# Order of VectorE and ScalarE work at the start of three feed-forward stages, and the first output rows scaled during the last chain of products

## The chip, the cores and the metric

One core of one Trainium2 chip runs the whole program. The metric is device time in microseconds (us); a kernel's time is the median of its runs.

## The reference, cut to what matters

A float32 model of three transformer blocks over one sequence of 256 tokens of width 1024. Each block is a mixer (stick-breaking attention, a latent attention with top-k selection, then sliding-window attention beside a gated recurrence) followed by a feed-forward stage, and the program ends with a norm over each token's row. The two places that the change touches:

```python
# feed-forward, blocks 0 and 1 (gate and val both pass the convolution)
h = rms_norm(x, norm_ffn[i]) * (1.0 + sc2) + sh2
u = h @ w_up                                   # 1024 -> 2 * 2816
y = conv_b + sum(up[:, j:j + S] * conv_w[j] for j in range(3))   # causal, along the tokens
gate, val = jnp.split(y, 2, axis=-1)
x = x + g2 * ((jax.nn.silu(gate) * val) @ w_down)
# block 2: only the gate passes the convolution
u, v = jnp.split(h @ w_up, 2, axis=-1)
x = x + gate_f * ((jax.nn.silu(causal_depthwise_conv(u, conv_w, conv_b)) * v) @ w_down)
return rms_norm_2(x, final_norm_g)             # y = x * rsqrt(mean(x * x) + EPS) * gain, row by row
```

## The kernel before

Activations lie transposed: xT holds 8 chunks of 128 channels by 256 tokens. Weights stream from HBM into six slots of 128 x 8 x 256 float32 (1 MB each), on SyncE's queue, in program order: the load of a slot waits for `slot_used` of that slot, and what stands behind it on the queue waits too. Every engine runs its own list of instructions, written out by hand and ordered by semaphores.

**Start of a feed-forward stage, `ffn(l)` for l = 0, 1, 2.** The output projection of the mixer before it (`out_projection`) makes eight chunks of xT in four blocks n = 0 to 3; `OUT_SLOTS[l]` names the slots of its four weight blocks. VectorE adds each block into xT, ScalarE makes xg (chunks of x times the gain, `xg_ready`) and squares, VectorE sums the squares (`sum_after_out`, ending in part_sum, `part_ready`). The first hidden columns don't wait for the norm: TensorE multiplies the unnormalised xg (`up_raw`, line 793, 64 matmul instructions) and in the midst of it adds up the squares over the partitions (`norm_sum`, line 760). From that ScalarE makes rstd (L1528, L1529), and VectorE multiplies the raw products by it afterwards (`normalise`, L2058 to L2063). In the meantime VectorE makes h from x (`norm`, L1978), ScalarE adds the shift (`shifted`, L1535, `h_ready`).

All later hidden columns are made from h in a fast form of 2 x 2 block products with seven products in place of eight (`up_seven`, L850). It needs sums of weights (`weight_sums(n, halves)`, four VectorE operations of 128 x 1024 at L2017, L2018, L2020, L2021: halves 0 are the first two, halves 1 the last two) and sums of inputs (`input_sums`, L2030 to L2036). Partial results lie in PSUM; ScalarE copies them on as starting values of the next products (`seed`, L1573, three per half step, and zeroing at L1590), and TensorE waits for each seed (`seeds_ready`). A step n has two half steps, j_odd 0 and 1; place p = 2n + j_odd numbers them, in tables `place_of`. After each half step VectorE adds two parts (`collect`, L2048), does the convolution (`chunk` on VectorE, L2081, L2086, L2091, `conv_ready`), ScalarE the silu (`chunk` on ScalarE, L1570, `silu_ready`), VectorE the product with the other half (`product`, L2106, L2111 or L2123). For l < 2 TensorE multiplies each such product by w_down at once (`down`, L896), 16 matmul instructions after every half step. For l = 2 the products are kept and multiplied at the end, in four blocks of seven chains (`down_blocks`, `chain`, L971, 22 matmul instructions each).

For l < 2 the first silu stands on ScalarE before the eight `shifted` operations, and the second between the first and the second seed of place 0. For l = 2 the first silu stands in the same place, the second after place 0. TensorE begins place 0 only when `normalise(1)` has read the second raw product (`was_read(3)`, a wait at the matmul of L865).

**The end.** VectorE adds each chain's result into xT (`take`, L2154). TensorE transposes finished pieces of xT back to rows (`turn`, L959, into PSUM banks 4 to 7), ScalarE squares and sums them row by row (`squares_of`, L1853, `ss_ready`), takes the root (`token_root`, L1860, `rtok_ready`), VectorE its reciprocal, and `token_rows` (L2666, 128 x 512 each) scales the rows by it and by the gain: three quarters of the output by VectorE, the third (rows 128 to 255, first half) by ScalarE (L1871). SyncE stores the four quarters (L598).

## Time and profile before

| what | value |
| --- | --- |
| median of 3 runs | 1099.87 us (1098.5 to 1101.79) |
| the profiled execution | 1098.37 us, of which the span from first to last instruction 1096.5 us |
| TensorE (PE) matmul busy | 1073.6 us, 98% of the span |
| VectorE (DVE) busy | 788.8 us, 72% |
| ScalarE (ACT) busy | 332.0 us, 30% |
| mean granted clock of TensorE | 0.999 of full speed |
| DMA | 234.79 MB, mean 214 GB/s |

A page of the profile gives busy time by engine and by group of instructions. Four other views are used below: the waits (which engine waited for which line, how long in total, how often, the longest), the timeline (instructions in order of time, like ones merged, with the idle time of their engine before them in brackets and what ended it), the windows (busy time of an engine in a stretch), and the chain of waits (the work that ended last, followed back). PEld is TensorE's weight load, which runs ahead of the matmul that it belongs to. SPq are DMAs issued by SyncE.

### The profile page before, as it was taken

Reading aid. Unit: us, or ns where it says so; the run is one execution under the profiler, and the core shown is the slowest. Engines: PE = TensorE matmul, PEld = TensorE weight load, DVE = VectorE, ACT = ScalarE, POOL = GpSimd, SP = SyncE. Lnnn points to the kernel's source line nnn. Section 1 sums busy time; section 2 is a strip of 40 time slices with the busy share of each in tenths; the row PEclk is TensorE's granted clock in tenths of the full one; section 3 lists DMA queues with packets and bytes.
Section 4 is the critical chain, followed back from the end, with each engine's and each line's share of the span. In section 5 each row is a group of like instructions: output and inputs, shape, how many; then the busy total and the mean of one; then the engine's idle time right before and its main releaser. Section 6 shows DMA issues by size and latency. Waiting matters only on the chain.

```text
span 1096.5 us, 18062 instructions
## 1 busy us (share of the span) xinstructions
PE 1073.6 (98%) x7396; PEld 972.1 (89%) x7396; DVE 788.8 (72%) x1359; ACT 332.0 (30%) x783; POOL 24.5 (2%) x83
## 2 busy tenths in 40 slices
PE   7999999999999999999999999999999999999997
PEld 4788888999999977888899999998889889999997
DVE  2477768888898848544779889887474288887755
ACT  3243324111111245663511111117343342222101
POOL 1000240000000000000000000000000000000000
PEclk9999999999999999999999999999999999999999
DMA  9899936898878662381868878774432165953411
GB/s 347 275 385 343 316 106 249 297 319 282 319 276 300 191 77 77 98 258 57 299 214 323 309 280 304 263 251 151 154 116 77 46 204 171 290 184 106 151 62 39
DMA packets 163011, 234.79 MB, mean 214 GB/s; under 512 B 8770, under 2 KB 137842, under 8 KB 162930
## 3 DMA queue, kind: packets, MB, share of 16 engines
q1 hardware_dynamic: 162572, 233.54, 63.2%
q8 instruction: 58, 0.95, 0.4%
q14 instruction: 24, 0.19, 0.1%
q10 hardware_dynamic: 357, 0.12, 0.0%
HBM read 232.19 MB, written 1.44 MB: 213 GB/s over the span
## 4 chain that ended last, share of the span: by engine, by line
PE 88%; DVE 8%; ACT 2%; issue 1%; ACTq 0%; DMA 0%; DVEq 0%
PE PS L850 34%; PE PS L780 13%; PE PS L896 13%; PE PS L808 7%; PE PS L971 6%; PE PS L1096 3%; PE PS L772 1%; PE PS L1358 1%; DVE hT L1978 1%; PE PS L793 1%; PE PS L701 1%; PE PS L1441 1%; DVE scratch L2400 1%; PE PS L1300 1%; PE PS L1049 1%
## 5 line engine op out<-in xcount | busy, mean ns | idle before, releaser
L780 PE MATMUL PS<-hT,slots 128*128 128x256 f32 x752 | 165.3, 380 | 0.8 <-ACT hT L1535 0.8
L780 PEld LDWEIGHTS PS<-hT,slots 128*128 128x128 f32 x752 | 142.1, 190 | 21.7 <-issue 2.9
L896 PE MATMUL PS<-act,slots 128*128 128x256 f32 x704 | 159.8, 380 | 0.4 <-DVE act L2123 0.4
L1902 DVE SCALAR_TENSOR_TENSOR ada_acc<-ada_slots,cond,ada_acc 128x1024 f32<-128x1024 f32 x119 | 152.4, 1280 | 4.8 <-DMA ada_slots<-in_ada_w 0.5
L896 PEld LDWEIGHTS PS<-act,slots 128*128 128x128 f32 x704 | 130.5, 190 | 18.9 <-issue 1.6
L1573 ACT ACTIVATE PS<-PS 128x128 f32<-128x128 f32 x180 | 53.5, 297 | 299.7 <-PE PS L850 299.7
L850 PE MATMUL PS<-oT,slots 128*128 128x128 f32 x960 | 126.9, 275 | 2.0 <-ACT PS L1573 2.0
L850 PE MATMUL PS<-hT,slots 128*128 128x128 f32 x960 | 127.0, 275 | 0.0
L850 PEld LDWEIGHTS PS<-hT,slots 128*128 128x128 f32 x960 | 119.6, 192 | 2.4
L850 PEld LDWEIGHTS PS<-oT,slots 128*128 128x128 f32 x960 | 116.8, 192 | 2.3 <-issue 2.3
L850 PE MATMUL PS<-oT,scratch 128*128 128x128 f32 x960 | 117.1, 275 | 0.0
L850 PEld LDWEIGHTS PS<-oT,scratch 128*128 128x128 f32 x960 | 112.0, 192 | 0.1
L808 PE MATMUL PS<-oT,slots 128*128 128x256 f32 x384 | 85.2, 380 | 0.0
L808 PEld LDWEIGHTS PS<-oT,slots 128*128 128x128 f32 x384 | 72.2, 190 | 10.7 <-issue 1.3
L850 PE MATMUL PS<-hT,scratch 128*128 128x128 f32 x480 | 63.4, 275 | 0.0
L850 PEld LDWEIGHTS PS<-hT,scratch 128*128 128x128 f32 x480 | 58.4, 192 | 0.0
L793 PE MATMUL PS<-xg,slots 128*128 128x257 f32 (+1 forms) x256 | 57.6, 381 | 0.0
L793 PEld LDWEIGHTS PS<-xg,slots 128*128 128x128 f32 (+1 forms) x256 | 47.7, 187 | 8.1 <-issue 0.8
L2081 DVE TENSOR_SCALAR ffn_work<-PS,pcol 128x256 f32<-128x256 f32 x100 | 50.7, 540 | 2.2
L1590 ACT ACTIVATE PS<-ident 128x128 f32<-128x128 f32 x60 | 16.6, 278 | 108.6 <-DVE PS L2048 108.6
L2048 DVE TENSOR_TENSOR PS<-PS,k_sq 128x256 f32<-128x256 f32 x54 | 23.2, 430 | 35.1 <-PE PS L850 33.4
L2086 DVE SCALAR_TENSOR_TENSOR ffn_work<-PS,pcol,ffn_work 128x255 f32<-128x255 f32 x100 | 44.2, 475 | 0.7
(347 smaller groups left out, 1337.0 us busy)
## 6 DMA issues: line engine op xcount, KB each, us to landing
ada_slots<-in_ada_w SPq DMA_DIRECT2D x144, 512.0 KB, 8.6
slots<-in_ffn_w_up SPq DMA_DIRECT2D x44, 1024.0 KB, 11.9
slots<-in_ffn_w_down SPq DMA_DIRECT2D x22, 1024.0 KB, 5.0
slots<-in_w_up SPq DMA_DIRECT2D x22, 1024.0 KB, 5.2
slots<-in_sb_w_in SPq DMA_DIRECT2D x11, 1024.0 KB, 13.2
slots<-in_w_in SPq DMA_DIRECT2D x11, 1024.0 KB, 5.3
slots<-in_dsa_w_in SPq DMA_DIRECT2D x10, 1024.0 KB, 5.4
ada_slots<-in_w_down SPq DMA_DIRECT2D x2, 2816.0 KB, 12.4
```

The costliest lines, as they stand in the source:

```text
L780: last = mm(PS[:, bank, half * T:half * T + T], slot[s][:, k, m * P:(m + 1) * P], x[:, k, :], start=k == 0, stop=k == KC - 1)
L793: last = mm(PS[0:n, bank, 0:T + 1], slot[s][:, k, m * P:m * P + n], xg[:, k, 0:T + 1], start=k == 0, stop=k == KC - 1)
L808: last = mm(PS[:, 2 * OUT_UNITS[l][n] + m, half * T:half * T + T], slot[OUT_SLOTS[l][n]][:, k, m * P:(m + 1) * P], oT[:, k, :], start=k == ...
L850: last = mm(dst, w[:, k, cols], x[:, k, :], start=fresh and k == 0, stop=k == HALF - 1, skip_group_check=True)
L896: last = mm(PS[:, c // 2, (c % 2) * T:(c % 2) * T + T], w[:, j_odd * D + c * P:j_odd * D + (c + 1) * P], act[:, j_odd, :], start=start and ...
L971: last = mm(PS[:, PRODUCT_BANKS[n % 4], 0:P], w[:, i, :], x[:, i, :], start=i == 0, stop=i == PAIRS - 1, skip_group_check=True)
L1096: last = mm(PS[:, 2 + tt, 0:SLAB], hT[:, k, tt * P:(tt + 1) * P], slot[s][:, k, :], start=k == 0, stop=k == KC - 1)
L1573: act_e.activation(dst.rearrange("p (x t) -> p x t", x=copies), stem(at).unsqueeze(1).to_broadcast([P, copies, P]), ACT.Copy).then_inc(see ...
L1902: ins = dve.scalar_tensor_tensor(dst, ada_slot[k][:, :], c, dst, ALU.mult, ALU.add)
L2048: dve.tensor_tensor(second, partial, at.z.unsqueeze(1).to_broadcast([P, 2, P]), ALU.add)\
L2081: dve.tensor_scalar(dst, ps[:, 0:T], dcol(f"conv2_{l}", j + off), dcol(f"convb_{l}", j + off), ALU.mult, ALU.add).then_inc(dve_step, 1)
L2086: dve.scalar_tensor_tensor(dst[:, 1:T], ps[:, 0:T - 1], dcol(f"conv1_{l}", j + off), dst[:, 1:T], ALU.mult, ALU.add).then_inc(dve_step, 1)
```

## The change

Three edits for the feed-forward starts, and one group for the end.

1. ScalarE, l < 2: the second silu of the stage (`chunk(1)`) moves from between the first and second seed of place 0 to behind its third seed. For l = 2 both first silus stand there, behind the eight `shifted` operations and the seeds of place 0.
2. VectorE, l = 2: the first half of `weight_sums(2, 0)` moves ahead of the last block of the output projection (`before_last`), the second half behind `sum_after_out`. Then `norm(1)` whole, `input_sums`, both `normalise` and `chunk`, the first half of `weight_sums(2, 1)`, both `product`. The third row of `OUT_SLOTS` changes from (2, 3, 4, 5) to (3, 4, 2, 5): slots 3 and 4, which hold the weights that `weight_sums(2, 0)` reads, are let go one block earlier.
3. TensorE, l = 2: the wait for the second `normalise` ahead of place 0 goes.
4. The end: TensorE transposes piece (7, 1) before the last three products of the last chain and no longer behind it. VectorE takes the first reciprocal and scales the first quarter before it takes the last chain, and adds up the square sums before it scales the second quarter. ScalarE issues the store of the quarter that it scales itself.

```diff
-OUT_SLOTS = ((3, 4, 5, 2), (3, 4, 5, 2), (2, 3, 4, 5))
+OUT_SLOTS = ((3, 4, 5, 2), (3, 4, 5, 2), (3, 4, 2, 5))
@@ SyncE, stores
-            for n, (made, count) in enumerate(((o_ready, 1), (o_ready, 2), (o_scaled, 1), (o_ready, 3))):
+            for count, n in enumerate((0, 1, 3)):
@@ TensorE, up_seven and down_blocks
-                    if n == 0 and not j_odd:
+                    if l < 2 and n == 0 and not j_odd:
                         was_read(3)
...
-                        if i == PAIRS - 1 and late is not None:
+                        if i == late_at and late is not None:
                             late()
...
+                def turn_corner():
+                    pe.wait_ge(x_turned, 11)
+                    pe.wait_ge(ss_ready, 3)
+                    turn(7, 1, signal=True)
...
-                    chain(b, 6, s_sum[2], acts[:, :, 1, P:T])
-                pe.wait_ge(x_turned, 11)
-                pe.wait_ge(ss_ready, 3)
-                turn(7, 1, signal=True)
+                    chain(b, 6, s_sum[2], acts[:, :, 1, P:T], late=turn_corner if b == 3 else None, late_at=8)
@@ ScalarE, ffn
-                chunk(0)
-                skip(2)
+                    chunk(0)
+                    skip(2)
                 shifted(3)
...
-                    if l < 2:
+                    if l < 2 and p:
                         chunk(1 - odd)
                         skip(3 - odd)
...
-                    if l == 2:
+                    if p == 0:
+                        for raw_odd in (0, 1) if l == 2 else (1,):
+                            chunk(raw_odd)
+                            skip(2 + raw_odd)
+                    elif l == 2:
                         chunk(1 - odd)
...
             act_e.activation(oT_flat[:, 1024:1536], oT_flat[:, 1024:1536], ACT.Copy, scale=rtok[:, 1:2]).then_inc(o_scaled, 1)
+            act_e.wait_ge(o_scaled, 1)
+            act_e.dma_start(out[0, P:2 * P, 0:512], oT_flat[:, 1024:1536]).then_inc(out_stored, 16)
@@ VectorE
                 for n in range(4):
+                    if n == 3 and before_last is not None:
+                        before_last()
...
+                        else:
+                            dve.wait_ge(rtok_ready, 1)
+                            link(dve.reciprocal(rtok[:, 0:1], rtok[:, 0:1]))
+                            token_rows(0, 0)
                         take(b, 6, (0, 1, 2))
...
+                if l == 2:
+                    weight_sums(2, 0, (1,))
+                    norm(1)
+                    input_sums()
+                    for odd in range(2):
+                        normalise(odd)
+                        chunk(odd, odd, raw[:, odd, 0, :], raw[:, odd, 1, :])
+                    weight_sums(2, 1, (0,))
+                    for odd in range(2):
+                        product(odd, normalised=True, j=odd)
+                    last_chunks()
+                    return
...
-            out_projection(2, units=OUT_UNITS[2])
+            out_projection(2, units=OUT_UNITS[2], before_last=lambda: weight_sums(2, 0, (0,)))
             ffn(2)
...
-            dve.wait_ge(rtok_ready, 1)
-            link(dve.reciprocal(rtok[:, 0:1], rtok[:, 0:1]))
-            token_rows(0, 0)
-            token_rows(0, 1)
             dve.wait_ge(ss_ready, 5)
             dve.tensor_tensor(ss[:, 1, 0:1], ss[:, 1, 0:1], ss[:, 1, 2:3], ALU.add).then_inc(ss_eps_ready, 1)
+            token_rows(0, 1)
```

ScalarE at the start of the first feed-forward stage, before: L1590 zeroes, L1573 are the seeds, L1596 copies the fifth product, L1570 is the silu.

```order
L1590 ACTIVATE PS<-ident 128x128 [waits unit_read2]
L1573 ACTIVATE PS<-PS 128x128 [waits stem_full0]
L1570 ACTIVATE ffn_work<-ffn_work 128x256 [waits conv_ready]
L1573 ACTIVATE PS<-PS 128x128 [waits stem_full0]
L1596 ACTIVATE k_sq<-PS 128x128
L1573 ACTIVATE PS<-PS 128x256 [waits stem_full0]
```

And the same place after the change, where lines stand two further down (L1572 is the silu).

```order
L1592 ACTIVATE PS<-ident 128x128 [waits unit_read2]
L1575 ACTIVATE PS<-PS 128x128 [waits stem_full0] x2
L1598 ACTIVATE k_sq<-PS 128x128
L1575 ACTIVATE PS<-PS 128x256 [waits stem_full0]
L1572 ACTIVATE ffn_work<-ffn_work 128x256 [waits conv_ready]
```

The silu went from between the seeds to behind them.

VectorE where the last feed-forward stage begins, before: L1995 adds the output projection into xT, L1952 sums squares, L2017 to L2021 are the weight sums, L2058 the first normalise.

```order
L1995 SCALAR_TENSOR_TENSOR xT<-PS,mod,xT 128x256 [waits unit_full0]
L1995 SCALAR_TENSOR_TENSOR xT<-PS,mod,xT 128x256
L1995 SCALAR_TENSOR_TENSOR xT<-PS,mod,xT 128x256 [waits unit_full1]
L1995 SCALAR_TENSOR_TENSOR xT<-PS,mod,xT 128x256
L1952 TENSOR_TENSOR hT<-hT 128x512 [waits sq_ready]
L1952 TENSOR_TENSOR hT<-hT 128x512 [waits sq_ready,dve_step] x2
L1952 TENSOR_TENSOR part_sum<-hT 128x256 [waits dve_step]
L2017 TENSOR_TENSOR scratch<-slots 128x1024 [waits w_sums_used,slot_loaded4,slot_loaded3]
L2018 TENSOR_TENSOR slots<-slots 128x1024 [waits dve_step]
L2020 TENSOR_TENSOR scratch<-scratch,slots 128x1024 [waits dve_step]
L2021 TENSOR_TENSOR scratch<-slots,scratch 128x1024 [waits dve_step]
L2058 TENSOR_TENSOR fm<-PS,rstd 128x256 [waits rstd_ready,unit_full2]
```

After the change (L2005 into xT, L1960 sums of squares, L2024 to L2028 weight sums, L1986 norm).

```order
L2005 SCALAR_TENSOR_TENSOR xT<-PS,mod,xT 128x256 [waits unit_full0]
L2005 SCALAR_TENSOR_TENSOR xT<-PS,mod,xT 128x256
L2024 TENSOR_TENSOR scratch<-slots 128x1024 [waits w_sums_used,slot_loaded4,slot_loaded3]
L2025 TENSOR_TENSOR slots<-slots 128x1024 [waits dve_step]
L2005 SCALAR_TENSOR_TENSOR xT<-PS,mod,xT 128x256 [waits unit_full1,dve_step]
L2005 SCALAR_TENSOR_TENSOR xT<-PS,mod,xT 128x256
L1960 TENSOR_TENSOR hT<-hT 128x512 [waits sq_ready]
L1960 TENSOR_TENSOR hT<-hT 128x512 [waits sq_ready,dve_step] x2
L1960 TENSOR_TENSOR part_sum<-hT 128x256 [waits dve_step]
L2027 TENSOR_TENSOR scratch<-scratch,slots 128x1024
L2028 TENSOR_TENSOR scratch<-slots,scratch 128x1024 [waits dve_step]
L1986 SCALAR_TENSOR_TENSOR hT<-xT,gain,rstd 128x256 [waits rstd_ready]
```

Two weight sums, with their wait for the loads of slots 3 and 4, now stand ahead of the last two additions into xT, and the norm stands ahead of the first normalise.

ScalarE behind the seeds of place 0 in that stage, after the change (before it, the table for the silu was loaded right behind the root, L1529):

```order
L1531 ACTIVATE rstd<-rstd 128x256 [waits act_step]
L1537 ACTIVATE hT<-hT,mod 128x256 [waits scaled_ready] x8
L1592 ACTIVATE PS<-ident 128x128 [waits unit_read1]
L1575 ACTIVATE PS<-PS 128x128 [waits stem_full0] x2
L1598 ACTIVATE k_sq<-PS 128x128
L1575 ACTIVATE PS<-PS 128x256 [waits stem_full0]
L1572 ACT_TABLE_LOAD
L1572 ACTIVATE ffn_work<-ffn_work 128x256 [waits conv_ready] x2
L1592 ACTIVATE PS<-ident 128x128 [waits unit_read2]
```

The table load and two silus now stand between place 0's last seed and the zeroing that place 1 waits for.

## Rows read from the trace of the kernel before

**Rows 1.** The waits, TensorE's own: us in total, times, longest

```profile
PE PS L850 <- ACT PS L1573: 2.0, 2, 1.0
...
PE PS L865 <- DVE cc L2059: 1.4, 1, 1.4
```

**Rows 2.** Timeline, first feed-forward stage, place 0: start, duration, engine, line

```profile
184.73 0.42 ACT L1570 ACTIVATE ffn_work<-ffn_work 128x256 f32<-128x256 f32 x1 [2.70 <-DVE ffn_work L2091]
...
185.19 0.43 DVE L2123 TENSOR_TENSOR act<-ffn_work 128x256 f32<-128x256 f32 x1
...
185.46 1.13 PE L850 MATMUL PS<-oT,slots 128*128 128x128 f32 x8 [1.05 <-ACT PS L1573]
...
188.10 3.33 PEld L896 LDWEIGHTS PS<-act,slots 128*128 128x128 f32 x16
```

**Rows 3.** Windows, place 0 of stages one and two, TensorE: stretch, length, busy, clock

```profile
180.56:191.66 11.10, 10.05 (x74) 1.00 0.22 71
543.04:554.07 11.03, 10.05 (x74) 1.00 0.22 68
```

**Rows 4.** Chain of waits, the next half step: start, duration, piece

```profile
191.94 6.25 PE PS L850 x56
198.19 3.46 PE PS L896 x16
```

**Rows 5.** Timeline, start of the last feed-forward stage

```profile
874.67 0.88 DVE L1995 SCALAR_TENSOR_TENSOR xT<-PS,mod,xT 128x256 f32<-128x256 f32 x2 [1.73 <-PE PS L808]
...
878.12 0.88 DVE L1995 SCALAR_TENSOR_TENSOR xT<-PS,mod,xT 128x256 f32<-128x256 f32 x2 [2.58 <-PE PS L808]
...
881.29 0.42 DVE L1952 TENSOR_TENSOR part_sum<-hT 128x256 f32<-128x256 f32 x1
881.63 1.22 DVE L2017 TENSOR_TENSOR scratch<-slots 128x1024 f32<-128x1024 f32 x1
...
882.25 0.59 PE L760 MATMUL PS<-part_sum,restart 128*128 128x256 f32 x2
...
893.81 0.22 PE L865 MATMUL PS<-ident_b 128*128 128x128 bf16 x1 [1.43 <-DVE cc L2059]
```

**Rows 6.** SyncE's timeline at the load of slot 3

```profile
871.64 0.37 SPq L437 DMA_DIRECT2D slots<-in_w_up  x1
```

**Rows 7.** DMA issues of that stretch: count, size, median us to landing

```profile
slots<-in_w_up SPq DMA_DIRECT2D x1, 1024.0 KB, 5.1
...
ada_slots<-in_final_norm_g SPq DMA_DIRECT2D x1, 512.0 KB, 8.9
```

**Rows 8.** Timeline, ScalarE and TensorE up to place 1 of the last stage

```profile
883.38 1.28 ACT L1529 ACT_TABLE_LOAD   x1
...
884.67 0.42 ACT L1529 ACTIVATE rstd<-rstd 128x256 f32<-128x256 f32 x1
...
898.73 0.37 ACT L1573 ACTIVATE PS<-PS 128x256 f32<-128x256 f32 x1 [1.34 <-PE PS L850]
...
899.32 0.27 ACT L1590 ACTIVATE PS<-ident 128x128 f32<-128x128 f32 x1
...
901.32 1.95 PE L850 MATMUL PS<-oT,scratch 128*128 128x128 f32 x16
```

**Rows 9.** Chain of waits, the end

```profile
1087.15 0.22 PE PS L959 x2
...
1089.86 0.36 DVE xT L2154
```

**Rows 10.** Timeline, the end: ScalarE, VectorE

```profile
1088.13 0.29 ACT L1860 ACTIVATE rtok<-ss 128x1 f32<-128x1 f32 x1
...
1090.56 1.41 DVE L2666 SCALAR_TENSOR_TENSOR oT<-PS,rtok,ada_slots 128x512 f32<-128x512 f32 x2
...
1092.13 0.29 ACT L1860 ACTIVATE rtok<-ss 128x1 f32<-128x1 f32 x1 [0.94 <-DVE ss L2674]
```

**Rows 11.** SyncE's timeline at the last two stores

```profile
1093.40 0.81 SPq L598 DMA_DIRECT2D out<-oT  x2
```

More of the change, by code:

```diff
@@ L593, in _ @@
                 load_down_block(b)
-            for n, (made, count) in enumerate(((o_ready, 1), (o_ready, 2), (o_scaled, 1), (o_ready, 3))):
+            for count, n in enumerate((0, 1, 3)):
                 tt, lo = n // 2, n % 2 * 512
-                sp.wait_ge(made, count)
+                sp.wait_ge(o_ready, count + 1)
                 sp.dma_start(out[0, tt * P:(tt + 1) * P, lo:lo + 512],
@@ L962, in turn, with chain @@
                         last.then_inc(turn_full, 1)
-                def chain(b, q, w, x, late=None):
+                def chain(b, q, w, x, late=None, late_at=PAIRS - 1):
                     n = 7 * b + q
@@ L2001, in out_projection, with weight_sums @@
                         after()
+            def weight_sums(l, n, halves=(0, 1)):
+                g, v = LAST_SETS[(n + 1) % 3] if l == 2 else (3 - 3 * (n % 2), 4 - 3 * (n % 2))
+                gate, val, ws = slot[g], slot[v], w_sum[n % 2]
+                if 0 in halves:
+                    for s, landed in zip((g, v), up_landed[l, n + 1]):
+                        dve.wait_ge(slot_loaded[s], landed)
+                    used = bk("w_sums_used")
+                    if used.n >= 2:
+                        dve.wait_ge(w_sums_used, used.value(1))
+                    used.next()
+                    link(dve.tensor_tensor(ws[:, 0, :, :], val[:, 0:HALF, :], val[:, HALF:KC, :], ALU.add))
+                    link(dve.tensor_tensor(val[:, 0:HALF, :], gate[:, 0:HALF, :], val[:, 0:HALF, :], ALU.subtract))
+                if 1 in halves:
+                    link(dve.tensor_tensor(ws[:, 1, :, :], ws[:, 0, :, :], gate[:, 0:HALF, :], ALU.subtract))
+                    dve.tensor_tensor(ws[:, 2, :, :], gate[:, HALF:KC, :], ws[:, 1, :, :], ALU.subtract)\
+                        .then_inc(w_sums_ready, 1)
@@ L2003, in ffn, with token_rows @@
+            def token_rows(tt, half):
+                lo = half * 512
+                dve.scalar_tensor_tensor(oT_flat[:, tt * D + lo:tt * D + lo + 512], PS[:, 4 + 2 * tt + half, :], rtok[:, tt:tt + 1],
+                                         final_g[:, lo:lo + 512], ALU.mult, ALU.mult).then_inc(o_ready, 1)
             def ffn(l):
                 both = l < 2
[L2006 to L2022 removed]
@@ L2054, in normalise @@
                     full(2 + odd)
-                    if not odd:
+                    if not odd and both:
                         dve.wait_ge(rstd_ready, bk("rstd_ready").next())
```

36 lines of the change are left out of this document (6 added, 30 removed).

## The prediction, made before the changed kernel was run

> **What bounds the kernel now.** I read TensorE's own waits first, because its matmuls fill nearly the whole span and every microsecond that it stands still is one that a reordering can give back. What is to be seen there is how little is left: the longest items that this change touches are 2.0 us in two waits of line 850 for a seed of ScalarE, and one of 1.4 us of line 865 for the second normalise on VectorE [rows 1]. Then the timeline around each of these, to see what the releasing engine did just before; and last the chain at the end of the program, where TensorE has finished and only short operations of VectorE and ScalarE, then the stores, follow one another. So the change can win at three starts of a stage and at the end, and each of these stands on the path: the stages between are TensorE's, and their loads are let go by TensorE's own progress, so what is won early should be kept.
>
> **Stages one and two (edit 1).** At place 0 of the first stage ScalarE makes its first seed, then waits 2.70 us for the convolution, does the silu from 184.73 on for 0.42 us, and only then the second seed; TensorE stands idle 1.05 us and goes on at 185.46 [rows 2]. The two waits together are 2.0 us [rows 1], so the second stage has about 1.0. With the silu behind the third seed the second one is made as soon as its product is there, and the wait goes. How much that is: at least the idle time, 1.05 and 1.0. At most the difference between this half step and an undisturbed one. The half step lasts 11.10 us in the first stage and 11.03 in the second [rows 3], an undisturbed one 6.25 + 3.46 = 9.71 [rows 4], which leaves 1.39 and 1.32, and in these lies the one small matmul of line 865 that only the first half steps have, some 0.1. The ends of matmuls in a profile are drawn late by the depth of the pipe, so the truth is between; I take 1.15 and 1.1.
>
> What is late next: the silu itself, and with it the product that the second `down` needs. The product before the third seed starts at about 184.3 in place of 185.46 and ends by about 185.4; the seed takes 0.37 (the same form as in [rows 8]), the silu 0.42, VectorE's product 0.43 with 0.04 of handing over [rows 2], together about 186.7. TensorE loads the first weights of `down` at 188.10 now [rows 2], then at 186.7 to 186.95. That is level to 0.2 us of slack. If I am a little wrong here it costs one or two tenths in each stage, no more, because the sum can't end later than this chain. VectorE has nothing else due in this gap.
>
> **Last stage (edits 2 and 3).** What goes is the wait for the second normalise, 1.43 us of idle TensorE before 893.81 [rows 5]; drawn late as above, up to 1.6. The next places take their banks one after another and don't need both normalises at once.
>
> What comes in its place is a wait on a load. The first two weight sums now stand ahead of the last two additions into xT. They need slots 3 and 4. With the new order of slots the load of slot 4 is issued when TensorE begins the third output block, which is when slot 3 is let go now, at 871.64 [rows 6]. It takes 5.1 us to land [rows 7], so it is there at 876.74. VectorE is free at 874.67 + 0.88 = 875.55 [rows 5], waits 1.2 us, and does two operations of 1.22 us with 0.04 between them [rows 5], until 879.3. Now the last additions start at 878.12. They start 1.2 us later. Behind them on VectorE are queued the sums of squares, and behind these TensorE's line 760; on ScalarE the last two chunks of xg, which TensorE's raw products eat one after another. The end of part_sum is at 881.29 + 0.42 = 881.71 and TensorE takes it at 882.25 [rows 5]: 0.54 of slack, of which some 0.15 is handing over. So 1.2 - 0.4 = 0.8 us of new idle time inside the raw products. All that follows from rstd fits well: the eight norms, eight shifts and four input sums are done some microsecond before TensorE has finished the raw products, because nothing of normalise or convolution stands between them any more.
>
> Then ScalarE. The table for the silu was loaded while it waited for VectorE; now it stands behind the last seed of place 0, with two silus behind it and then the zeroing without which TensorE can't make the second product of place 1. From TensorE's start at 893.81: the last seed ends at 898.73 + 0.37 = 899.10, which is 5.3 us after it; a table load is 1.28 and the next operation starts 0.01 after it (883.38 to 884.67) [rows 8]; two silus at 0.42 each and the zeroing 0.27, the last overlapping somewhat: 5.3 + 1.3 + 0.7 + 0.3 = 7.6. TensorE wants it at 901.32 - 893.81 = 7.5 [rows 5, 8], less the handing over of about 0.15 to 0.2. A new wait of about 0.3. VectorE is not late there: two times normalise and convolution are done before the table is.
>
> Sum of the stage: 1.5 - 0.8 - 0.3 = 0.4 us. Its bounds are 1.6 (neither new wait) and below nothing, -0.5 (the load a microsecond later than 5.1).
>
> The Trainium skill, "ScalarE: Activation LUTs", section "What ACT_TABLE_LOAD costs", says that a switch of table takes about 1.38 us of draining beside its 1.28, 2.66 us in all. By that the new wait would be 1.7 and not 0.3, the stage would lose 1.0 and the sum below would be 2.2. The row speaks against it: the operation behind the load starts 0.01 us after its 1.28 [rows 8], and I go by the row.
>
> **The end (edit 4).** The square sums of the last piece are there at 1092.13 - 0.94 = 1091.19, but the root starts only at 1092.13, because VectorE first scales two quarters (1.41 us from 1090.56) and then adds up the sums that the root needs [rows 10]. After the change the first quarter is scaled while the last chain runs: its root is started at 1088.13 and takes 0.29, reciprocal and scaling fit before VectorE takes the last chain at 1089.86 [rows 9, 10]. The sum stands ahead of the second quarter, and that quarter is done before the next reciprocal. So 0.94 goes, less 0.05 of handing over from the squares. Against it the transposition inside the last chain puts the chain's end 0.11 later (two take 0.22 [rows 9]); half of that is returned because the squares of that piece are no longer what the last transposition waits for. Net 0.85. The two last stores are issued in 0.81 us from 1093.40 on, one behind the other [rows 11]; with ScalarE issuing one, the fourth is up to 0.4 sooner, at worst nothing if their data share the engines anyhow. I take 0.1, nearer nothing, since two quarters still have to pass.
>
> **The sum.** 1.15 + 1.1 + 0.4 + 0.85 + 0.1 = 3.6 us. The profiled execution, 1098.37 us with a span of 1096.5, becomes 1094.8 with a span of 1092.9. That execution is 1.5 us below the median of the runs shown, and within their spread; taken off the median: 1099.87 - 3.6 = 1096.3 us, or 0.33%. A measurement of this kernel can tell about 0.3%, 3.3 us, from no change.
>
> **Rivals.**
> - *No new wait in the last stage* (slot 4 lands before VectorE is free, or table and silus hide): for it, all three are a matter of tenths; against it, the load is issued too late by 1.2 us unless TensorE runs the blocks differently. 1.15 + 1.1 + 1.5 + 0.95 = 4.7, so 1095.2 us. Chance 0.10.
> - *The last stage gives more back than it wins.* The zeroing of place 1 waits for a table load that can't run ahead. If switching holds ScalarE a microsecond longer than the row of the load itself, or VectorE's second convolution is late, the stage ends at -1.0: gain 2.2, 1097.7 us. For it: 0.3 us is already missing by my own count, and every tenth more goes straight onto TensorE. Chance 0.15.
> - *The early gain isn't kept.* In stages one and two the silu is late for `down` and the wait only moves there, or a later piece that hangs on loads takes it back: only the end is won, and little more, gain about 1.3, 1098.6 us. For it: the slack of 0.0 to 0.2. Against it: the old wait was for something ready only at 184.73, and the new chain ends two microseconds later but 1.4 us before TensorE's present 188.10. Chance 0.18.
> - *Slower: the load of slot 4 is late.* VectorE is an engine in order, and with the weight sums ahead of the additions into xT every microsecond by which that load lands later than 5.1 stops TensorE for a microsecond. It decides from 5.1 + 3.6 = 8.7 us on. There is a row for that: a load of half the size issued on the same queue while others were under way took 8.9 [rows 7]; it would give +0.2 us, 1100.1. Against it: at 871.64 the queue is empty, since what stands ahead was issued one block earlier. Chance 0.05.
> - The forecast itself: 0.52.
>
> **How the numbers follow.** The forecast's own span is a gain of 2.7 to 4.5, 1095.4 to 1097.2; of its 0.52 about 0.40 lies over 3.3. Faster by over 0.3%: 0.40 + 0.10 = 0.50. Within 0.3%: 0.12 + 0.15 + 0.18 = 0.45. Slower: 0.05, half of it past 0.3% by the row, all of it counted. The range takes in the first three rivals and the scatter of a median of a few runs, whose single runs lie 1.4 us below and 1.9 above the present one: 1094.6 to 1099.2.
>
> **What would show it right or wrong.** In TensorE's waits the two of line 850 for the seed are gone, and no wait of `down` for VectorE's product has come at its place; half step 0 of the first two stages lasts 9.8 to 9.9 us. In the last stage the wait for the normalise is gone, VectorE's first weight sum there starts about 1.2 us after it is free and names the load as its releaser, TensorE idles about 0.8 us in the raw products, and 0.2 to 0.4 us at place 1 for ScalarE's zeroing, with the table load directly ahead. At the end the second root starts within 0.1 us of the last squares, and the last scaling ends 0.85 us sooner after the last chain. Wrong, if TensorE's idle time at place 1 is over a microsecond, if the first weight sum waits more than 2 us, or if the sum of these places is right and the time doesn't follow.

## The result, and the profile after

The changed kernel takes 1094.01 us (median of 4 runs, 1093.74 to 1094.63) where the kernel before takes 1099.69 beside it (4 runs, 1098.5 to 1101.79). The ratio is 0.9947, with a 95% interval of 0.993 to 0.9964: faster by 0.53%. The prediction was 1096.3 us with a range from 1094.6 to 1099.2. The direction is right, the gain is larger than forecast, and the time lies 0.6 us below the range. Two of all the runs counted below were far off (one of e1 at 1119.86 us with a granted clock of 0.948, one of the kernel before at 2882.23 us); the ratios leave them out and the medians hardly feel them.

The profiled execution took 1093.74 us with a span of 1091.9. TensorE is busy for 1071.2 us of it (1073.6 before).

TensorE's waits after, longest first (us in total, times, longest). The two of line 850 for a seed and the one of line 865 for the second normalise [rows 1] are gone: the list goes on with waits of 1.1 us and less, none of them of lines 850 or 865.

```profile
PE PS L1030 <- DMA oT<-in_x: 3.6, 1, 3.6
PE PS L1021 <- DMA ffn_work<-in_c: 3.0, 1, 3.0
PE PS L1037 <- DMA ffn_work<-in_ffn_norm_g: 1.7, 1, 1.7
PE PS L721 <- DVE mod L1946: 1.2, 1, 1.2
```

The timeline of place 0 in the first feed-forward stage (start, duration, engine, line), to be held against [rows 2]:

```profile
184.89 0.37 ACT L1575 ACTIVATE PS<-PS 128x256 f32<-128x256 f32 x1 [1.34 <-PE PS L850]
185.17 0.41 ACT L1572 ACTIVATE ffn_work<-ffn_work 128x256 f32<-128x256 f32 x1
...
185.58 1.06 PE L850 MATMUL PS<-oT,slots 128*128 128x128 f32 x8
185.61 0.42 DVE L2139 TENSOR_TENSOR act<-ffn_work 128x256 f32<-128x256 f32 x1 [0.97 <-ACT ffn_work L1572]
186.37 0.73 PEld L896 LDWEIGHTS PS<-act,slots 128*128 128x128 f32 x4
```

The silu (line 1572) now stands directly behind the third seed (line 1575), and VectorE's product ends at 186.03, 0.34 us before TensorE loads the first weights of `down`. So nothing waits there. The windows of the same half step, which answer to [rows 3] (stretch, length, then TensorE's busy time):

```profile
180.12:189.93 9.81, 9.81 (x74) 9.31 (x73) 8.13 (x19) 1.68 (x6) 0.00 (x0) 1.00 0.24 75
541.31:551.13 9.82, 9.82 (x74) 9.31 (x73) 8.07 (x19) 1.68 (x6) 0.00 (x0) 1.00 0.25 79
```

TensorE is busy in the whole of both, and they are 1.29 and 1.21 us shorter than before.

The timeline at the start of the last stage, which answers to the first rows of [rows 5]:

```profile
873.84 1.22 DVE L2024 TENSOR_TENSOR scratch<-slots 128x1024 f32<-128x1024 f32 x1 [1.23 <-issue]
...
874.98 4.85 PE L793 MATMUL PS<-xg,slots 128*128 128x257 f32 x20
875.10 1.22 DVE L2025 TENSOR_TENSOR slots<-slots 128x1024 f32<-128x1024 f32 x1
...
876.35 0.88 DVE L2005 SCALAR_TENSOR_TENSOR xT<-PS,mod,xT 128x256 f32<-128x256 f32 x2
...
877.82 1.60 PEld L793 LDWEIGHTS PS<-xg,slots 128*128 128x128 f32 x8 [0.48 <-ACT xg L1551]
...
880.00 0.70 PE L760 MATMUL PS<-part_sum,restart 128*128 128x256 f32 x2 [0.17 <-DVE part_sum L1960]
```

VectorE is idle for 1.23 us ahead of its first weight sum, which the view puts down to "issue". The chain of waits has the load of slot 4 right ahead of it (start, duration, piece):

```profile
868.70 3.91 DMA slots<-in_w_up
872.61 1.23 issue
873.84 1.24 DVE scratch L2024
...
876.35 0.04 DVE xT L2005
```

From the issue at 868.70 to VectorE's start at 873.84 it is 5.14 us, and that load took 5.1 us to land (the four of this stretch 5.0 to 5.2). So VectorE waited for the load, though the view doesn't name it. The additions into xT (line 2005) then start 1.37 us after TensorE's first raw product; before they started 0.20 us after it (878.12 in [rows 5], against this line of the timeline before):

```profile
877.92 4.50 PE L793 MATMUL PS<-xg,slots 128*128 128x257 f32 x20
```

TensorE pays at two places. Its weight loads wait 0.48 us for ScalarE's xg, and the row of 20 matmuls takes 4.85 us in place of 4.50. Then it waits for part_sum, so that line 760 starts 5.02 us after the first raw product and no longer 4.33 (882.25 - 877.92). The other new wait is at place 1 (the same timeline, further on), against [rows 8]:

```profile
894.84 0.37 ACT L1575 ACTIVATE PS<-PS 128x256 f32<-128x256 f32 x1 [1.34 <-PE PS L850]
...
895.23 1.28 ACT L1572 ACT_TABLE_LOAD   x1
...
896.43 0.22 PE L865 MATMUL PS<-ident_b 128*128 128x128 bf16 x1
...
896.52 0.72 ACT L1572 ACTIVATE ffn_work<-ffn_work 128x256 f32<-128x256 f32 x2
...
897.15 0.26 ACT L1592 ACTIVATE PS<-ident 128x128 f32<-128x128 f32 x1
897.47 2.05 PE L850 MATMUL PS<-oT,scratch 128*128 128x128 f32 x16
```

The table load, two silus and the zeroing (line 1592) follow each other without a gap, and TensorE starts the product behind the zeroing 0.98 us after the eight before it (896.49), where one place earlier it is 0.95, and its 16 matmuls take 2.05 in place of 1.95. That is the whole of the new wait.

The end, timeline, against [rows 9, 10, 11]. The store is ScalarE's own (ACTq):

```profile
1084.90 0.75 DVE L2034 SCALAR_TENSOR_TENSOR oT<-PS,rtok,ada_slots 128x512 f32<-128x512 f32 x1
...
1086.22 0.35 DVE L2170 SCALAR_TENSOR_TENSOR xT<-PS,mod,xT 128x128 f32<-128x128 f32 x1 [0.57 <-PE PS L971]
...
1087.22 0.19 ACT L1859 ACTIVATION_READ_ACCUMULATOR hT<-PS 128x1 f32 x1
1087.45 0.29 ACT L1866 ACTIVATE rtok<-ss 128x1 f32<-128x1 f32 x1
...
1087.98 0.75 DVE L2034 SCALAR_TENSOR_TENSOR oT<-PS,rtok,ada_slots 128x512 f32<-128x512 f32 x1
1088.73 0.39 ACTq L1879 DMA_DIRECT2D out<-oT  x1
```

The first quarter is scaled before the last chain is taken, and the second root starts 0.04 us after the sum of its squares has been read out (1087.22 + 0.19), with no idle bracket. Before, it started 0.94 us late [rows 10].

**Where the gain sits.** The first half steps of a stage each begin with a small matmul of line 865, and the distances between the starts of these differ between executions by a hundredth or two. Only where a load is waited for do they differ more: the 15.09 of the third row is 15.15 in e4, and 15.26 and 15.24 in e7 and e10, which have the same program there. So the trace gives the gain of each part nearly free of the scatter of whole times (us; a "place" is such a start):

| from, to | before | after | gain |
|---|---|---|---|
| stage one, place 0 to 1 | 11.10 | 9.81 | 1.29 |
| stage two, place 0 to 1 | 11.03 | 9.82 | 1.21 |
| last stage, first raw product to place 0 | 15.89 | 15.09 | 0.80 |
| last stage, place 0 to 1, and 1 to 2 | 6.50, 6.37 | 6.36, 6.50 | 0.01 |
| the pair of turns in the last chains, to the span's end | 9.34 | 8.50 | 0.84 |
| stage one, place 0, to the span's end | 915.93 | 911.78 | 4.15 |

The change is worth 4.15 us in the traces, against 3.6 in the prediction, and the medians lie 5.7 apart. The first question of the experiments is what the other 1.5 us are.

### The profile page after: what moved, and what is told of

It is laid out like the page before. It is cut to its first block, busy times and chain, and to the rows that moved or that the text cites. A ratio compares the mean times of both kernels' runs of the same rounds, so it can differ in the third digit from the quotient of the medians.

```text
span 1091.9 us, 18061 instructions
## 1 busy us (share of the span) xinstructions
PE 1071.2 (98%) x7396; PEld 971.0 (89%) x7396; DVE 789.0 (72%) x1359; ACT 331.9 (30%) x783; POOL 23.9 (2%) x83
## 3 DMA queue, kind: packets, MB, share of 16 engines
HBM read 232.19 MB, written 1.44 MB: 214 GB/s over the span
## 4 chain that ended last, share of the span: by engine, by line
PE 88%; DVE 5%; SPq 4%; ACT 1%; DMA 1%; issue 1%; DVEq 0%
PE PS L850 34%; PE PS L896 13%; PE PS L780 12%; PE PS L808 6%; PE PS L971 6%; PE PS L793 4%; PE PS L1098 2%; SPq L437 2%; PE PS L1360 1%; SPq L447 1%; PE PS L701 1%; SPq L504 1%; PE PS L1443 1%; DVE scratch L2428 1%; DMA ada_slots<-in_ada_w 1%
```

## The experiments

In each, "the places" are the distances of the table above, and the range behind a ratio is its 95% interval. Times of the kernel before, run beside the changed ones on the same chip, are given with each group.

**Parts 1 to 4: each part alone, and all again.** The kernel before beside these took 1098.97 us (median of 27 runs).

e1 is the kernel before with only the silu of place 0 moved behind the seeds in stages one and two:

```diff
-                    if l < 2:
+                    if l < 2 and p:
                         chunk(1 - odd)
                         skip(3 - odd)
...
+                    if l < 2 and p == 0:
+                        chunk(1)
+                        skip(3)
```

> Edit 1 alone (the second silu of stages one and two behind the third seed). Theory A, the sum of places: in the trace of the changed kernel TensorE is 1.29 us ahead after place 0 of stage one and 1.22 after that of stage two, so this kernel alone is 2.5 us faster than before and place 0 of both stages lasts 9.8 us from start to start. Theory B, something beside the places: the measured gain of the whole change is 5.7 us by the medians and the places show 4.2, so one of its parts carries 1.5 us more than its place shows; if it is this one, the time falls by 4 us while the places show 2.5.

Measured: 1096.39 us (11 runs), ratio 0.9975 (0.9966 to 0.9985), 2.6 less than before. The half steps are 9.82 and 9.82 us, stage one to the span's end 913.45 (2.48 less). The last stage is that of before, its wait included. This part holds more than half of the gain of the places, and it is kept to the end of the program.

e2 is the changed kernel with the first part and the end put back, so only the last stage is new (order of slots, weight sums ahead of the last additions, both input sums and normalises in a row, no wait for bank 3):

```diff
-OUT_SLOTS = ((3, 4, 5, 2), (3, 4, 5, 2), (2, 3, 4, 5))
+OUT_SLOTS = ((3, 4, 5, 2), (3, 4, 5, 2), (3, 4, 2, 5))
...
-                    if n == 0 and not j_odd:
+                    if l < 2 and n == 0 and not j_odd:
                         was_read(3)
...
+            out_projection(2, units=OUT_UNITS[2], before_last=lambda: weight_sums(2, 0, (0,)))
```

> Edits 2 and 3 alone (order of VectorE and ScalarE at the start of the last feed-forward stage, slot order, TensorE's wait gone). Theory A: 0.8 us faster, TensorE 0.8 ahead at place 2 of that stage, with a wait of VectorE for the load of slot 4 of about 1.2 us and idle time of TensorE of about 0.65 us in the raw products. Theory B, if this part carries the remainder: 2.3 us faster with 0.8 at the place.

Measured: 1097.87 us (11 runs), ratio 0.9997 (0.9988 to 1.0006), the median 1.1 less than before. By the ratio that is no clear difference; by the places, which tell more here, stage one to the span's end is 915.15, 0.78 less.

e3 is the kernel before with only the end changed (first quarter and turn inside the last chain, sum ahead of the second quarter, one store from ScalarE):

```diff
-                    chain(b, 6, s_sum[2], acts[:, :, 1, P:T])
+                    chain(b, 6, s_sum[2], acts[:, :, 1, P:T], late=turn_corner if b == 3 else None, late_at=8)
...
+                            token_rows(0, 0)
...
+            act_e.dma_start(out[0, P:2 * P, 0:512], oT_flat[:, 1024:1536]).then_inc(out_stored, 16)
```

> Edit 4 alone (the end: corner transposed inside the last chain, first quarter scaled early, square sums first, one store issued by ScalarE). Theory A: the last scaling ends 0.9 us earlier after the last chain and the span is 0.8 us shorter, since the time from the last scaling to the end of the program is 0.1 longer than before. Theory B, if this part carries the remainder: 2.3 us faster with 0.8 at the place.

Measured: 1097.55 us (11 runs), ratio 0.999 (0.9981 to 0.9999), the median 1.4 less. Stage one to the span's end is 915.04, 0.89 less. The three parts add up in the places: 2.48 + 0.78 + 0.89 = 4.15, the same as all together. None of them takes from another.

e4 is the changed kernel once more, with no line edited.

> The changed kernel once more, unaltered. Theory A: the places give 4.2 us and the rest of the 5.7 us between the medians is the scatter of the start (before 160 us the one profiled execution of before was 0.45 us behind that of the changed kernel, with the first 40 products at half the pace), so with more runs the difference settles at 4 to 4.6 us. Theory B: it stays at 5.5 us or more, and something beside the places is faster in every run.

Measured: 1094.2 us (5 runs), ratio 0.9962 (0.9949 to 0.9975), 4.8 between the medians and 4.2 by the ratio; stage one to the span's end 911.79. The changed kernel came back at its time, and the kernel before did not: its median was 1099.87 of the three runs shown and 1099.69 of the first four, but 1098.97 of these 27, 1098.58 of ten and 1098.63 of nine later on. So about 1 us of the 5.7 was a few high runs of the kernel before. Some 0.5 us are left: the later runs of before have a median of 1098.66 us (45 runs, without the one far off), the nine of the changed kernel 1094.10, which is 4.56 apart. The runs' spans, from first to last instruction, are 1096.4 and 1092.3 us in the median, 4.1 apart, which agrees with the places. The rest lies outside the span. In those 45 runs the time is longer than the span by 1.72 to 2.87 us (median 2.41), in the nine by 1.70 to 1.90. It goes with the end: in e3's 11 runs it is 1.75 to 1.85, while in e1 and e2, which have the old end, it goes up to 2.80 and 2.47. Issuing a store from ScalarE isn't the reason, since with all stores on SyncE (e7, below) it is 1.72 to 1.80 in four runs. Which other part of the new end does it stays open; no trace shows what lies outside the span.

**The two new waits of the last stage.** The kernel before beside these took 1098.58 us (10 runs).

e5 is the changed kernel with all four operations of the first weight sums behind the sums of squares:

```diff
-                    weight_sums(2, 0, (1,))
+                    weight_sums(2, 0)
...
-            out_projection(2, units=OUT_UNITS[2], before_last=lambda: weight_sums(2, 0, (0,)))
+            out_projection(2, units=OUT_UNITS[2], before_last=None)
```

> The changed kernel with one part put back: all four operations of the first weight sums of the last stage stand behind the sums of squares, so that nothing waits for slot 4 ahead of the last additions into xT. Theory A (the raw products lose their time to the load): VectorE's last additions start about 1.2 us earlier, TensorE's distance from the first raw product to the half step at place 0 falls from 15.09 to about 14.4 us (-0.6 to -0.8). Theory B (what holds the raw products is the order of ScalarE and the sums themselves, and the load only happens to lie beside them): the distance stays within 0.15 of 15.09. Either way the second VectorE operation of norm comes up to 1.5 us later and may be missed at place 1: if so the distance from place 0 to place 1 goes from 6.36 to 6.5 or more. One look, no timing; the distances between places hardly differ between executions.

Measured: from the first raw product to place 0 it is 14.30 us, 0.79 less than in the changed kernel; place 0 to 1 stays at 6.36 and place 1 to 2 at 6.50. One run took 1093.47 us. The timeline shows why: the additions start 0.20 us after TensorE's first raw product, as before, and neither wait is left in the 20 products.

```profile
875.65 4.50 PE L793 MATMUL PS<-xg,slots 128*128 128x257 f32 x20
875.85 0.88 DVE L2005 SCALAR_TENSOR_TENSOR xT<-PS,mod,xT 128x256 f32<-128x256 f32 x2 [2.58 <-PE PS L808]
...
879.98 0.38 PE L760 MATMUL PS<-part_sum,restart 128*128 128x256 f32 x1
```

The two weight sums by themselves would have been out of the way in time: without the wait they end at 876.32 - 1.23 = 875.09 us in the changed kernel, and the additions are due at 874.98 + 0.20. So theory A holds, waiting for the load cost 0.79 us (up to 0.96 by the executions of e7 and e10), and that VectorE's weight sums now end 8.71 us after the first raw product in place of 7.37 costs nothing.

e6 is e5 with ScalarE's table of the silu loaded ahead of the first seed of the last stage:

```diff
                     chunk(0)
                     skip(2)
+                else:
+                    act_e.preload_act_table(ACT.Silu)
                 shifted(3)
```

> As the one above (the first weight sums behind the sums of squares), and ScalarE loads the table for the silu before the first seed of the last stage, in place of between the last seed of place 0 and the first silu, where TensorE waits for the zeroing behind them. Theory A (both new waits are what I named): 0.6 to 0.8 us less in the raw products and 0.1 to 0.2 less at place 1, so place 2 comes 0.7 to 0.95 us sooner after the first raw product than in the changed kernel (27.95 us there), and the time is 0.7 to 1.0 us below it, near 1093.4 where before is 1098.5 to 1099. Theory B (the table load, 1.28 us, can't be hidden anywhere in ScalarE's row, it only delays the first seed): place 0 takes over 0.3 us longer than in the one above, and the time is within 0.3 us of the changed kernel.

Measured: first raw product to place 0 14.30 us, then 6.36 and 6.36; in all 0.93 less than the changed kernel. Time 1093.47 us (5 runs, 1092.88 to 1094.26), ratio 0.9955 (0.9942 to 0.9967). ScalarE now has 1.59 us to spare behind the zeroing, where it had 0.22:

```profile
894.52 0.75 ACT L1572 ACTIVATE ffn_work<-ffn_work 128x256 f32<-128x256 f32 x2
...
895.18 0.26 ACT L1594 ACTIVATE PS<-ident 128x128 f32<-128x128 f32 x1
...
897.03 0.26 ACT L1575 ACTIVATE PS<-PS 128x128 f32<-128x128 f32 x1 [1.59 <-PE PS L850]
```

Theory A holds by the places: the table's wait at place 1 was worth 0.14 us, the load's wait 0.79. By the places this is also the best version run, 5.14 us below the kernel before (stage one to the span's end 910.79). The median of the times is 0.5 to 0.7 below the changed kernel's (1094.01 and 1094.2), less than the 0.7 to 1.0 expected and within the scatter of the start.

**The slower rival, with its price.** e8 is the changed kernel with the old order of slots, so that slot 4 is let go one block later:

```diff
-OUT_SLOTS = ((3, 4, 5, 2), (3, 4, 5, 2), (3, 4, 2, 5))
+OUT_SLOTS = ((3, 4, 5, 2), (3, 4, 5, 2), (2, 3, 4, 5))
```

> The changed kernel with the old order of slots in the third output projection (2, 3, 4, 5), so that slot 4 is let go one output block later (about 3.45 us by the profile of before), while its weight sums still stand ahead of the last additions. This is the slower rival at its full price. Theory A (TensorE pays for each microsecond by which the load comes later than VectorE is free): VectorE's wait ahead of the first weight sum grows from 1.23 to about 4.7 us, and TensorE's distance from the first raw product to place 0 from 15.09 to about 18.5 us. Theory B (TensorE has other raw work beside it that hides a part): the wait grows as said, the distance by less than 2.5 us. One look, no timing.

Measured: VectorE waits 4.86 us ahead of the first weight sum, 3.63 more than in the changed kernel. From the first raw product to place 0 it is 19.97 us, 4.88 more. The wait came as theory A said, but both theories priced the distance too low. One run took 1099.1 us; stage one to the span's end is 916.64, 0.71 more than before. So the rival was real: with that one tuple left as it was, the change would have been no gain by the places. The timeline and the windows (length, TensorE and weight loads busy, ..., granted clock third from the end) show where the 1.25 us beyond the longer wait come from:

```profile
878.11 1.23 DVE L2024 TENSOR_TENSOR scratch<-slots 128x1024 f32<-128x1024 f32 x1 [4.86 <-issue]
...
882.10 2.78 PE L793 MATMUL PS<-xg,slots 128*128 128x257 f32 x8 [3.72 <-ACT xg L1551]
```

```profile
880.00:882.00 2.00, 0.00 (x0) 0.00 (x0) 1.96 (x4) 0.46 (x2) 0.00 (x0) 1.00 1.10 347
882.00:883.00 1.00, 0.90 (x4) 0.78 (x5) 0.79 (x2) 0.98 (x4) 0.00 (x0) 1.00 1.10 349
883.00:884.00 1.00, 1.00 (x5) 0.80 (x4) 0.90 (x2) 1.00 (x1) 0.00 (x0) 0.59 1.10 396
884.00:885.00 1.00, 1.00 (x4) 0.79 (x3) 1.00 (x2) 0.27 (x1) 0.00 (x0) 0.50 0.50 197
...
886.00:887.00 1.00, 1.00 (x5) 0.86 (x4) 0.61 (x1) 0.98 (x2) 0.00 (x0) 0.70 0.00 0
```

After 3.72 us of idle time TensorE was granted 0.50 of its clock, the 1.2 GHz level, from about 883.4 to 886.6, while it was already at work again. These eight products took 2.78 us, where the same eight took 2.00 in e4.

**The wait that was removed.** e9 is the kernel before with only the wait for bank 3 gone, VectorE's order untouched. The kernel before beside it and beside the next two took 1098.63 us (9 runs).

```diff
-                    if n == 0 and not j_odd:
+                    if l < 2 and n == 0 and not j_odd:
                         was_read(3)
```

> The kernel before with one thing gone: in the last stage TensorE doesn't wait at place 0 for bank 3, the bank of the second normalise. Everything else, the order of VectorE and ScalarE too, is that of before. Theory A (the 1.43 us wait is an order of waiting, and can be dropped by itself): the distance from the first raw product to place 0 falls from 15.89 to about 14.4 us, and the time is 1.4 us below before. Theory B (VectorE's order, where the second normalise comes behind the first convolution, makes the wait come back one step on, at the second product of place 0 or at place 1): place 2 comes less than 0.7 us sooner after the first raw product than before (28.76 us). If B holds, the new order of VectorE was needed to keep the gain.

Measured: the first raw product to place 0 falls to 14.30 us, 1.59 less; place 0 to 1 rises to 8.09, 1.59 more. To place 2 it is 28.75 us against 28.76. One run took 1098.65 us. TensorE's timeline and VectorE's:

```profile
891.80 0.22 PE L865 MATMUL PS<-ident_b 128*128 128x128 bf16 x1
894.46 2.02 PE L850 MATMUL PS<-oT,scratch 128*128 128x128 f32 x16 [1.49 <-DVE oT L2030]
```

```profile
892.42 0.75 DVE L2058 TENSOR_TENSOR fm<-PS,rstd 128x256 f32<-128x256 f32 x2
...
893.66 0.69 DVE L2030 TENSOR_TENSOR oT<-hT 128x512 f32<-128x512 f32 x1
```

Theory B holds. The wait for the second normalise stood in front of one for the input sums (line 2030), which VectorE makes only behind that normalise. In the changed kernel they come at 886.14, ahead of both normalises. With that order the 1.59 us are a gain (e5); removing the wait alone gives nothing.

**The store.** e7 is the changed kernel with all four stores on SyncE:

```diff
-            act_e.wait_ge(o_scaled, 1)
-            act_e.dma_start(out[0, P:2 * P, 0:512], oT_flat[:, 1024:1536]).then_inc(out_stored, 16)
```

> The changed kernel with all four output stores on SyncE again, in the order of before. Theory A (the two last stores end together whoever issues them; the prediction's 0.1 us isn't there): from the end of the last scaling to the end of the span 3.05 to 3.2 us, as the 3.17 of the changed kernel and the 3.09 of before. Theory B (a second issuing engine is worth what I gave it): 3.25 to 3.6 us. The time is no help here, since the difference looked for is 0.1 us.

Measured: 1093.98 us (4 runs). The last scaling starts here and is over at 1089.92, and the span ends at 1093.0:

```profile
1089.17 0.75 DVE L2032 SCALAR_TENSOR_TENSOR oT<-PS,rtok,ada_slots 128x512 f32<-128x512 f32 x1
```

From there to the span's end it is 3.08 us, against 3.17 in the changed kernel, 3.11 in e4 and 3.09 before. The second issuing engine is worth nothing here.

**The start.** Within the span, only the stretch ahead of stage one differs by microseconds between executions (place 0 of stage one came at 179.98 to 182.56 us in thirteen profiled ones). In the kernel before the first 40 products of the adaLN weights take 4.45 us, in the changed one 2.37, in e4, which has the same program, 3.91. e10 is the changed kernel with 13 unused products in TensorE's first waits; e11 is e6 with 5 and 3 of them in place of 9 and 4:

```diff
+            warm(9)
             pe.wait_ge(x_loaded, 32)
...
+            warm(4)
             pe.wait_ge(params_loaded, 16 * len(FIRST_ROWS))
```

> The changed kernel with 13 products more, of the identity and unused results, in TensorE's two first waits (9 before x has landed, 4 before the parameters have). The first 40 products of the adaLN weights took 4.45 us in some profiled executions (the one of before among them) and 2.37 in others, and the start is the only part in which executions of one kernel differed by more than 0.2 us. Theory A (the pace of these products hangs on whether TensorE stood idle just before): they take 2.4 us, the first place of stage one comes at 180.1 us or sooner, the median is 0.5 to 1.5 us below the changed kernel's 1094.0 to 1094.2 and the runs lie closer together. Theory B (the start is set by when the small loads land, which differs from run to run whatever TensorE does): no difference over 0.3 us in the median, and the same spread of about 1 us.

> The candidate for the best kernel: the changed kernel with the weight sums behind the sums of squares and the silu's table ahead of the first seed (it measured 1093.47 us), and at the start 5 unused products before x has landed and 3 before the parameters have, fewer than the 9 and 4 that held x back by 2.8 us. Theory A (TensorE's pace at the start hangs on whether it worked before, and this is what the runs differ by): the transposition of x takes 1.9 us as in the run with 9 and 4, in place of 3.3 to 3.7, the first 40 products 2.4 us, the place of stage one comes at 179.9 to 180.2 us, the median is 1092.7 to 1093.1 with a spread under 1 us. Theory B (landings set the start): the median is within 0.3 us of 1093.47 and the spread is 1.4 us as there, or wider.

Measured: e10 1093.7 us (6 runs, 1093.62 to 1096.56; four within 0.08, two 2.9 higher), ratio 0.9966 (0.9953 to 0.9978). e11 1093.86 us (5 runs, 1092.76 to 1094.54), ratio 0.9956 (0.9944 to 0.9969), no better than e6's 1093.47. The pace did answer: the 16 transpositions take 1.91 us in both, where the eleven others have 3.34 to 3.68, as e11's timeline shows:

```profile
3.03 4.36 PE L1024 MATMUL PS<-ident 128*128 128x256 f32 x10
7.23 1.91 PE L1035 MATMUL PS<-ident,oT 128*128 128x128 f32 x16
...
12.53 0.42 PE L1043 MATMUL PS<-ident,ffn_work 128*128 128x128 f32 x2 [2.09 <-DMA ffn_work<-in_ffn_norm_g]
12.88 3.65 PE L1057 MATMUL PS<-ada_slots,cond 128*32 128x256 f32 x40
```

But then the parameters were still to come: TensorE was idle for 2.09 us, its granted clock was 0.50 from 14 us on, and the 40 products took 3.65 us. So each theory has a part. The transpositions are faster when TensorE worked before, and it wins nothing, since the parameters that land later end the wait. What sets the pace of the 40 products isn't settled: behind transpositions of 3.68 and 3.67 us and idle times of 1.35 and 1.44 they took 2.37 us in e2 and 3.91 in e4. Why the parameters land at 11.5 us in one execution and at 13.3 in another stays open too.

## Why the prediction was partly wrong

The mechanisms came as forecast, but for the store. The time was 2.3 us too high: 1.2 of it by the base that the gain was taken off, 0.55 by the sum of the gains, and about 0.5 by time outside the span.

- **The base: the step that failed most.** I took 3.6 off the median of three runs, 1099.87, though I had noted that the profiled run lay 1.5 lower. The later runs put the kernel before at 1098.6 to 1099.0 (1098.66 over all), 1.2 us lower. With 1098.6 to 1099.0 the same sum gives 1095.0 to 1095.4, and with the 4.15 of the places 1094.4 to 1094.8.
- **Outside the span: a term put at nothing.** I let the time fall by just as much as the span. The runs show about 0.5 us more (e4, above), which comes with the new end and is in no trace. With it the 1094.4 to 1094.8 become 1093.9 to 1094.3, and 1094.01 was measured.
- **Stages one and two: mechanism right, size too small.** I had the upper bounds of 1.39 and 1.32 less 0.1 for the one matmul of line 865, which is 1.29 and 1.22, and took 1.15 and 1.1 because a wait's bracket showed 1.05. The runs gave 1.29 and 1.21. The bracket shows less than the stall: an undisturbed row of eight matmuls is drawn 1.06 us long (186.42 in the kernel before), yet the next row starts 0.89 us after it (187.31), so some 0.17 of a stall lies under the drawn end. The comparison with an undisturbed half step was exact. Missing: 0.25 us. That the silu would then be about level with `down` was right; the slack is 0.34 us, and I had up to 0.2.
- **Last stage: both new waits were there, one priced right, and this is the term most mis-sized: 0.4 against 0.80.** The stall was 1.59 (15.89 - 14.30), where I took 1.5 and gave 1.6 as the most. The load's cost was predicted at 0.8 and is 0.79 (e5), VectorE's wait at 1.2 and is 1.23. The wait behind the table was predicted at 0.3 and is 0.14 (e6). And before the change, place 0 to 1 took 0.14 more than the undisturbed 6.36, for the first of the input sums, which ends just as TensorE needs it (894.09 + 0.69, against 894.88); I had not seen that, and it went too. 1.59 - 0.79 + 0.14 - 0.14 = 0.80 us.
- **The table load.** The 1.38 us of draining beside the load that the Trainium skill, "ScalarE: Activation LUTs", section "What ACT_TABLE_LOAD costs", gives don't show: the load starts 0.02 us behind the seed (894.84 + 0.37 to 895.23), and the silu 0.01 us after the load's 1.28 us (896.52).
- **What I did not ask of the last stage** is what stands behind the removed wait. I credited the gain to "the next places don't need both normalises at once". e9 shows that without the new order of VectorE this gives 0.01 us. The input sums, which I named only in passing as done in time, carry it.
- **The end: 0.84 in place of 0.95.** The waiting root went as forecast (0.94 late before, 0.04 now). The 0.1 for the store was nothing (e7), and I had called it nearer nothing.
- **The range.** Its low end, 1094.6, was 5.3 below the base. That held all parts at their upper bounds (1.29 + 1.22 + 1.6 + 0.95 = 5.06), but next to nothing for a base that was itself too high, though one of its three runs lay 1.4 lower and the profiled one 1.5.
- **The slower rival** was right in kind and too cheap: I had it paying a microsecond for a microsecond, and it pays 4.88 for 3.63 (e8). The granted clock of 0.50 behind the long wait fits the difference of 1.25; no run has the wait without the lower clock.

## What to carry to other kernels

Price a stall by the difference from the same step where nothing waits, not by the bracket in front of an instruction: the bracket said 1.05 where 1.29 was to be had. When a wait is to be removed, look up what the same engine needs next and when the engine behind it makes that: dropping the wait alone gave 0.01 us, with the reordering it gave 1.59. And when an operation that waits for a load is pulled ahead in an engine that works in order, everything queued behind it starts after that load. If it must stand there, the order in which buffers are let go has to follow, as the one tuple of slots does here (4.88 us); better here was to leave it behind (e5, 0.79 us).

For a change of half a per cent, three whole times are a poor base. Distances between fixed matmuls in the trace repeated to 0.02 us, and to 0.17 where a load is waited for, while whole times of one kernel differ by 2. But a whole time holds more than the span: compare time less span between the kernels too, since here 0.5 us of the gain is found only there.

## What the runs showed of the hardware that was not expected

TensorE's granted clock falls to 0.50 (1.2 GHz) in its work behind an idle time of some microseconds: after 3.72 us it was at 0.50 from about 883.4 to 886.6 (e8), after 2.09 us from 14 us on (e11). Shorter waits left it at 1.00: 0.5 us in the raw products of the changed kernel, 1.43 us ahead of place 0 in the kernel before, 1.49 us in e9. In the first microseconds of this program the view's clock doesn't tell the pace: the same 40 products take 4.45 us and 2.37 us in stretches that both show 1.00 (length, matmuls with their count, ..., clock third from the end; the kernel before, then the changed one), and only the count of matmuls tells them apart.

```profile
12.00:14.00 2.00, 2.00 (x21) 0.99 (x24) 0.46 (x2) 1.98 (x2) 0.00 (x0) 1.00 1.03 414
```

```profile
12.00:14.00 2.00, 2.00 (x38) 1.16 (x41) 0.47 (x2) 1.98 (x2) 0.00 (x0) 1.00 1.03 422
```
